# One prompt pair loaded a stage earlier, one row tile of two projections loaded without a free buffer, and the last stores split over two queues

## What is computed

```
# layer 0
qa, ka, va, za, qb, kb, vb, zb = split(rmsnorm(x) @ w_in_even)     # 3584 columns
oa = dilated sliding-window attention(qa, ka, va)    # 8 heads of 64, causal; prompt, and sample over a cache
ob = retention(rotary(qb), rotary(kb), vb)           # 4 heads
x  = x + concat(oa * silu(za), head_norm(ob) * silu(zb)) @ w_out_even
# layer 1
q, kc, vc, ks, vs, kw, vw, gl, z = split(rmsnorm(x) @ w_in_odd)    # 2864 columns
o  = gated sum of compressed, selected and window attention(q, ...)   # 16 heads
x  = x + (o * silu(z)) @ w_out_odd
y  = rmsnorm(x)
```

## Time and profile before

| what | value |
|---|---|
| median of three runs | 1970.13 us |
| the profiled execution, its own time | 1969.05 us |
| span of its instructions | 1967.3 us |
| TensorE busy | 95% of the span, 13566 matmuls |
| VectorE, ScalarE, GpSimd busy | 44%, 36%, 20% |
| DMA | 254.06 MB, 129 GB/s on average |
| mean granted TensorE clock | 0.978 of 2.4 GHz |

### The profile page before, as it was taken

How to read it: one execution, slowest core, us unless ns; L and a number is a source line. 1 busy time by engine, 2 the same in 40 slices (tenths; PEclk the granted TensorE clock), 3 DMA queues, 4 the chain that set the end, 5 groups by cost and what they waited for, 6 DMA issues and landing times. The chain is left out here.

```text
span 1967.3 us, 35219 instructions
## 1 busy us (share of the span) xinstructions
PE 1878.1 (95%) x13566; PEld 1449.7 (74%) x13566; DVE 865.5 (44%) x2575; ACT 699.5 (36%) x1527; POOL 390.6 (20%) x552
## 2 busy tenths in 40 slices
PE   7999999798998999999999999999899999999898
PEld 6777777576876888788885555565688778788787
DVE  5222221576555353212411121212677777777534
ACT  5100000464332231001003323322567676776522
POOL 0000000000751000000022113110355555555200
PEclk9999999899997999999989999999899999999999
DMA  5443442663788653844345143250400000000464
GB/s 206 163 145 128 147 142 72 217 192 104 251 274 262 196 199 120 257 168 146 85 177 191 44 151 119 76 151 12 124 23 23 7 23 24 23 13 7 156 203 144
DMA packets 158532, 254.06 MB, mean 129 GB/s; under 512 B 33858, under 2 KB 109824, under 8 KB 154016
## 3 DMA queue, kind: packets, MB, share of 16 engines
q1 hardware_dynamic: 144480, 206.25, 32.3%
q0 software_dynamic: 4608, 33.56, 4.8%
q10 hardware_dynamic: 9280, 12.00, 2.0%
HBM read 205.85 MB, written 52.96 MB: 132 GB/s over the span
## 5 line engine op out<-in xcount | busy, mean ns | idle before, releaser
L1717 POOL TENSOR_SCALAR sparse_pr<-sparse_pr,sparse_coef,sparse_gate 128x63 f32<-128x63 f32 (+8 forms) x384 | 247.2, 666 | 206.9 <-DVE sparse_coef L1671 206.8
L1059 PE MATMUL x_acc<-x_w_hi,x_y_lo 128*128 128x478 f32 (+3 forms) x768 | 274.9, 358 | 2.4 <-DVE x_y_lo L907 2.4
L1059 PE MATMUL x_acc<-x_w_lo,x_y_hi 128*128 128x478 f32 (+3 forms) x768 | 269.2, 350 | 0.0
L1059 PE MATMUL x_acc<-x_w_hi,x_y_hi 128*128 128x478 f32 (+3 forms) x768 | 268.7, 350 | 0.0
L2865 PE MATMUL ss_ps_h<-ss_xT,cmp_w 128*128 128x508 f32 x512 | 244.0, 594 | 0.8 <-ACT ss_xT L2707 0.8
L1613 ACT ACTIVATE sparse_pr<-sparse_pr,sparse_nmax 128x63 f32<-128x63 f32 (+8 forms) x384 | 227.4, 597 | 2.8 <-DVE sparse_nmax L1665 2.8
L447 PE MATMUL h_acc<-h_w_hi,h_y_lo 128*128 128x512 f32 x448 | 177.6, 396 | 0.8 <-DVE h_y_lo L372 0.8
L447 PE MATMUL h_acc<-h_w_hi,h_y_hi 128*128 128x512 f32 x448 | 174.8, 390 | 0.0
L447 PE MATMUL h_acc<-h_w_lo,h_y_hi 128*128 128x512 f32 x448 | 174.8, 390 | 0.0
L1059 PEld LDWEIGHTS x_acc<-x_w_hi,x_y_lo 128*128 128x128 f32 x768 | 145.7, 190 | 29.2 <-issue 14.7
L1059 PEld LDWEIGHTS x_acc<-x_w_hi,x_y_hi 128*128 128x128 f32 x768 | 145.6, 190 | 11.3
(11 more groups left out here) (383 smaller groups left out, 2667.8 us busy)
## 6 DMA issues: line engine op xcount, KB each, us to landing
h<-h_out SPq DMA_DIRECT2D x56, 256.0 KB, 2.1
h_w_side<-in_even_w_in SPq DMA_DIRECT2D x16, 896.0 KB, 5.0
h_w_raw<-in_even_w_in SPq DMA_DIRECT2D x6, 2048.0 KB, 7.9
x_w_side<-in_odd_w_in SPq DMA_DIRECT2D x16, 716.0 KB, 4.7
cmp_lent<-in_odd_w_in SPq DMA_DIRECT2D x5, 1912.0 KB, 9.1
h<-x_out SPq DMA_DIRECT2D x40, 239.0 KB, 2.2
ev_unit<-in_cache_a_k SPq DMA_DIRECT2D x4, 2048.0 KB, 8.4
ev_unit<-in_cache_a_v SPq DMA_DIRECT2D x4, 2048.0 KB, 12.1
```

The lines of the kernel that those rows point to most:

```text
L1059: last = nc.tensor.matmul(acc[b][:, 0:passes[p][3]], left[:, k, t * P:(t + 1) * P], weights(right, p)[:, k, :], start=(k == 0 and a == 0), ...
L1717: nc.gpsimd.tensor_scalar(row, row, one, gate[:, t, 2 * i + e, (br + 1) % 3:(br + 1) % 3 + 1], ALU.mult, ALU.mult).then_inc(scaled, 1)
```

## The change

- **First pair.** Queries, keys and values of the first dilated pair and the table of constants are loaded within `project`, by SyncE, behind the second store of the last chunk, once the stores of chunks 0 to 2 have landed. They go into a memory (`cmp_lent`) that the projection doesn't use. Two probability buffers of the dilated stage that lay there have tiles of their own now, and `oT` and `o_sb` of that stage move into the memory that held the constants.
- **Third row tile.** In both output projections row tile 2 is loaded into `held[2]` and `held[3]`, with a semaphore of its own (`third_in`), and without a wait, as the first thing that SyncE does. Tile 4 then waits for tile 0 to be turned, not for tile 2.
- **Last stores.** In both `attend_prompt` the last group is copied out in pieces with a semaphore for each (`out_done`), and its four stores go out two by SyncE and two by ScalarE (`store_last`).
- **Warm calls.** `project` and both `attend_prompt` begin on ScalarE with one activation of 128x1 (Sqrt, Exp) whose result isn't used.

```diff
+class FirstPair:
+    def __init__(self, nc, ctx, constants, h):
+        self.lent = ctx.enter_context(nc.sbuf_tensor("cmp_lent", [P, 2 * PAST], F32))
+        part = [self.lent[:, m * T:(m + 1) * T] for m in range(4)]
+        self.q_in, self.k_in, self.v = (x.rearrange("p (t c) -> p t c", t=NT) for x in part[0:3])
+        self.con, self.con_in = constants(ctx, "dilated", part[3]), sem("con_in")
...
+    def load(self, sp):
+        for to, col, loaded in ((self.q_in, QA, self.q_loaded), (self.k_in, KA, self.kv_loaded), (self.v, VA, self.v_loaded)):
+            sp.dma_start(to, self.hp[:, :, col:col + P]).then_inc(loaded[0], 16)
+        self.con.load(sp, self.con_in)
...
                     for t in range(NT):
                         store(i, t)
+                        if i == n_chunks - 1 and t == 1:
+                            n_needed = -(-pair.last_column // chunk) * NT
+                            for b in range(3):
+                                sp.wait_ge(stored[b], 16 * ((n_needed - b + 2) // 3))
+                            pair.load(sp)
...
                 act.wait_ge(eps_ready, 1)
+                nc.scalar.activation(warm[:, :], eps[:, :], ACT.Sqrt)
...
         def loads_of(t):
-            return t // 2 * 16 * len(gates)
+            if t == 2:
+                return third_in, 16 * len(gates)
+            return loaded[t % 2], (t // 2 - (1 if t % 2 == 0 else 0)) * 16 * len(gates)
+
+        def x_of(t):
+            return held[2] if t == 2 else x[:, t % 2, :]
+
+        def z_of(t):
+            return held[3] if t == 2 else z[:, t % 2, :]
...
                 def load_gated(t, n):
-                    b = t % 2
-                    if t >= 2:
-                        sp.wait_ge(turned[b], t // 2)
-                    sp.dma_start(x[0:n, b, :], rows(src, t, n)).then_inc(loaded[b], 16)
+                    done = loads_of(t)[0]
+                    if t > 2:
+                        sp.wait_ge(turned[t % 2], 1 if t == 4 else t // 2)
+                    sp.dma_start(x_of(t)[0:n, :], rows(src, t, n)).then_inc(done, 16)
...
+        def store_last(eng, m):
+            i, t, at = units[4 * last_group + m][0:3]
+            eng.wait_ge(out_done, at % 4 + 1)
+            eng.dma_start(mix[t * P:(t + 1) * P, i * P:(i + 1) * P], o_sb[last_group % 2][:, at % 4, :]).then_inc(stored[last_group % 2], 16)
...
                     ins = nc.vector.tensor_scalar(to[:, c0:c0 + HD], src[:, c0:c0 + HD], coef[u % N_COEF][:, e:e + 1], None, ALU.mult)
-                ins.then_inc(bank_free[entry_of[what, x] % RING], 1)
+                    if x == last_group and e == 1:
+                        ins.then_inc(out_done, 1)
...
+            if what == "out" and x == last_group:
+                for m in range(4):
+                    nc.vector.tensor_copy(to[:, m * P:(m + 1) * P], src[:, m * P:(m + 1) * P]).then_inc(out_done, 1)
...
-                    load_pair(sp, 0)
-                    con.load(sp, con_in)
                     load_pair(sp, 1)
-                    load_v(sp, 0)
                     load_v(sp, 1)
...
+                    if g == last_group:
+                        for m in (0, 2):
+                            store_last(sp, m)
+                        continue
...
+                nc.scalar.activation(warm[:, :], con("ident")[:, 0:1], ACT.Exp)
...
+                for m in (1, 3):
+                    store_last(act, m)
```

More of the change, by code:

```diff
@@ L555, in project_out @@
         gain_in, eps_ready = sem("gain_in"), sem("eps_ready")
-        loaded = [sem(f"loaded{b}") for b in range(2)]
+        loaded, third_in = [sem(f"loaded{b}") for b in range(2)], sem("third_in")
         opened = first if early is None else early
@@ L1041, in turn @@
                         pe.wait_ge(yT_written[b], u)
[L1042 removed]
+                    fr = z[:, t % 2, :] if second else x_of(t)
                     for k in range(KD):
[L1044 removed]
+                        last = nc.tensor.transpose(tps[b][:, k, 0:n], fr[0:n, k * P:(k + 1) * P], ident[0:n, 0:n])
                     last.then_inc(turned[b], 1)
@@ L1343, in attend_prompt @@
         else:
-            con, con_in = constants(ctx, kind, outer.constants), sem("con_in")
-            q_in = [sb(f"q_in{b}", [P, NT, P]) for b in range(2)]
+            con, con_in = outer.pair.con, outer.pair.con_in
+            q_in = [outer.pair.q_in, sb("q_in1", [P, NT, P])]
         qT = [sb(f"qT{b}", [P, T]) for b in range(2)]
-        if sparse:
-            pr = [sb(f"pr{b}", [P, 2, rows[b % 2]]) for b in range(UB)]
-        else:
-            pr = [outer.wide[b // 2][:, 0:2 * rows[0]].rearrange("p (e c) -> p e c", e=2) if b in (0, 2) else
-                  sb(f"pr{b}", [P, 2, rows[b % 2]]) for b in range(UB)]
+        pr = [sb(f"pr{b}", [P, 2, rows[b % 2]]) for b in range(UB)]
         prT = [sb(f"prT{b}", [P, 512]) for b in range(N_T)]
+        warm = sb("warm", [P, 1])
         nmax = [sb(f"nmax{b}", [P, NC]) for b in range(UB)]
@@ L1356, in attend_prompt @@
         coef = [sb(f"coef{b}", [P, NC]) for b in range(N_COEF)]
-        oT = [sb(f"oT{b}", [P, 512]) for b in range(2)]
-        o_sb = [sb(f"o{b}", [P, 4, P]) for b in range(2)]
+        if sparse:
+            oT = [sb(f"oT{b}", [P, 512]) for b in range(2)]
+            o_sb = [sb(f"o{b}", [P, 4, P]) for b in range(2)]
+        else:
+            oT = [outer.z[:, 0, b * 512:(b + 1) * 512] for b in range(2)]
+            o_sb = [outer.z[:, 1, b * 512:(b + 1) * 512].rearrange("p (t c) -> p t c", t=4) for b in range(2)]
         if sparse:
```

50 lines of the change are left out of this document (28 added, 22 removed).

## The result

| | before | after |
|---|---|---|
| median of six runs | 1968.83 us (1965.8 to 1970.44) | 1952.92 us (1950.6 to 1959.13) |
| profiled execution, own time | 1969.05 us | 1950.6 us |
| its span | 1967.3 us | 1948.7 us |
| its mean granted clock | 0.978 | 0.981 |

The ratio is 0.9923, with a 95% interval of 0.991 to 0.9937: 0.77% faster, 15.9 us between the medians. The spans of the two profiled executions lie 18.6 us apart; the profiled one of after is the fastest of its six.

What follows compares the result with a forecast made beforehand. TensorE is busy in 95% of the span, so time is won only where it stands still or runs at the lower clock. Terms 3.9 + 0.8 + 2.2 + 7.1 + 3.5 = 17.5 us off 1969.05 gave 1952 us, range 1949 to 1955.5.

Steps and rivals of the forecast that it cites:

- One sign that the prediction named for being wrong: Output projections: a wait for DMA-fed rows before tile 3 or 5 would show the prediction wrong.
- first pair: Dilated start: early loads let TensorE start 3.56 us earlier and remove a 0.31 us keys wait; together 3.9 us.
- warm calls: Dilated start: the 1.28 us table load moves to the barrier; 0.8 us, bounds 0 and 1.28; kernel and sparse starts 0.
- last stores: Ends of both attention stages: two queues and stores by quarters save 1.3 us (dilated) and 0.9 us (sparse), 2.2 together.
- first projection: First output projection: waits of 1.84 and 2.06 us and 3.4 of slow clock go, less 0.2: 7.1 us.
- TensorE starts at about 349.73: Dilated start: with the data already there, TensorE starts right behind the barrier, 3.56 us earlier.
- about 6 us of work run at half clock: Dilated start: slow work worth 3 us if the clock returned at once, as much the other way if later; taken as 0.
- It just fits: First output projection: at 5.8 us of load, tile 5 is in at 634, and TensorE needs it at 634.2.
- no wait, no fall ... 1.7 us lost each: First output projection: without its two waits the clock stays up, saving 1.7 us at each, 3.4 in sum.
- The waits did move in part: Rival: the output projections' waits move to the next tile, half of 10.6 us comes, gain 12.2, 1957 us; chance 0.2.
- The dilated stage gave nothing back: Rival: dilated stage starts earlier but gives it back, bound by ScalarE and VectorE; gain 12.8, 1956 us; chance 0.07.
- The loads in flight together: Slower rival: loads of tile 3, tile 4 and weights share engines, tile 3 lands last; 1971 us or more; chance 0.03.

Runs made afterwards that it cites:

- number 1: Changed kernel, but the first dilated pair and its constants are loaded behind the barrier again: 1959.78 us, ratio 0.9951 to the kernel before.
- number 4: Changed kernel without the three small activations that load a table early: 1953.62 us, ratio 0.9918 to the kernel before.
- number 5: Changed kernel, but both output projections ask for the second weights behind tile 5, not ahead of it: 1957.48 us, ratio 0.9948 to the kernel before.
- number 9: Kernel before, with only the third row tile of both output projections loaded early: 1962.06 us, ratio 0.9953.
- the fill: Changed kernel plus 14 unread TensorE products behind the first projection's last product: 1950.92 us, ratio 0.9918; run again, 1952.79 us, 0.9912.

## Why the prediction was right, and where a term was not

Forecast 1952, measured 1952.92. The sum was 17.5 us from the trace. By the measured stretches it should have been 16.2 (the front 5.4, which holds the first two terms of the table, and the others as they stand there), and the medians are 15.9 apart. That the forecast comes within 1 us is in part luck: 2.6 us too much in the first projection stood against 1.1 us that was in no term and 0.4 of the first pair. One sign that the prediction named for being wrong did come: a wait for loaded rows before tile 5, 1.64 us. The time was right, and that step of its reasoning was not.

| term | forecast | measured | from |
|---|---|---|---|
| first pair | 3.9 | 4.3 | front, number 1 |
| warm calls | 0.8 | 0.7 to 1.2 | number 4; fronts before (27.2) and of number 1 |
| last stores | 2.2 | 2.0 | 5.54 to 4.12, 4.68 to 4.10 |
| first projection | 7.1 | 4.5 | first pass |
| second projection | 3.5 | 3.2 | its stretch to the end |
| wait ahead of the first projection | none | 1.1 | chance, below |

*First pair.* The step "TensorE starts at about 349.73" came out in its mechanism, with the barrier as releaser, but 3.98 us behind the last product and not 3.6: the warm calls cost that 0.32 us (number 4). The clock's share was put at 0 with bounds of 3 us, and within them it is a draw. Seven fronts of the same work spread over 2.4 us, and the order follows the clock, which is low in them for 3.4 us (the shortest) to 10.2 (the four longest). The reading "about 6 us of work run at half clock" was short: before, the clock fell only 2.3 us into the gap, so 4.9 of the 13.7 low us were idle and 8.8 were work. Not foreseen was that a gap of 4 us can leave the turns at 2.4 GHz.

*Warm calls.* I took 0.8 between 0 and 1.28, on the ground that another engine would take some of the 1.04 us. None did; the size is right because the later barrier takes 0.32 us back, which was not foreseen. The drain that the Trainium skill, "ScalarE: Activation LUTs", section "What ACT_TABLE_LOAD costs", adds to the load would have made the term 1.4 larger. The trace of number 4 speaks against it: without the warm call the load is back, and what returns in TensorE's waits is 1.04 us, less than even the load's own 1.28. The start of the kernel gave 0, as argued from the waits for DMA: the first product starts at 14.89 without and at 14.93 with the call.

*Last stores.* The size was right, and part of the reason wrong. I counted issue times of two queues and an earlier start as if they added up. They replace each other: 0.65 and 1.16 us by themselves at the dilated end, 1.42 together; 0.61 and 0.35 at the sparse end, 0.58 together. At the sparse end the four copies last 0.89 us and the single one 0.69, and VectorE has other work behind them that ends 0.8 us ahead of the barrier; that this eats the earlier start is argued and not shown.

*First projection: the term that was mis-sized.* Two steps failed. "It just fits" for tile 5: the load took 7.6 us and not 5.8, since the weights ahead of it were still on their way, and number 5 shows that this lateness passes to whatever tile stands behind them. An earlier issue doesn't help it: the changed kernel issued tile 5 13.9 us behind the pass's first turn and its repetition 16.0 us, and both times its silu began 21.5 us behind that turn. And "no wait, no fall ... 1.7 us lost each": the clock did stay up where the waits had been, but the 3.4 us were added as if TensorE set the pace alone. It doesn't here. The first pass of the changed kernel lasts 39.50 us with the clock low for its first 2.8 us and a wait of 1.64, and in its second run 39.52 us with the clock low for 9.1 us and no wait for rows at all. Where the clock is high TensorE meets the late tile, where it is low the tile is there. The ten profiles with the early third tile and the old place of the weights order themselves so: low for 2.8 us, wait 1.64; 4.3, 1.33; 4.4, 1.14; 7.9, 0.90; 8.2 to 9.1 in the six others, none. In eleven profiles with the early third tile the first pass lasts 39.1 to 40.4 us, 39.7 in the mean; without it 44.78 and 43.66. So 2.6 of the 7.1 us were not there to be won.

```profile
605.00:615.00 10.00, 9.35 (x39) 0.55 0.90 303
615.00:625.00 10.00, 10.00 (x72) 1.00 0.94 323
```

These are windows of the second run of the changed kernel: 0.55 of the clock with the transfers at a share of 0.90, and then full clock beside a share of 0.94.

*What was not in the sum.* The wait ahead of the first output projection is 2.66 us in the profiled execution. In the ten others that have the changed kernel's dilated end, or nearly so, it is 2.94, 3.07, 3.12, 3.31, 3.36, 3.84, 3.96, 4.18, 4.60 and 5.19, and in the two of the old kernel's kind 4.87 and 4.59. No edit orders these numbers, but the stage's last eight issues do, the stores of the sample states: where they took 8.8 to 9.7 us the wait is 2.7 to 3.4, where they took 10.0 to 10.4 it is 3.8 to 5.2 (before and number 9 among these), and TensorE starts 4.0 to 4.2 us behind the end of the last issue in twelve of the thirteen profiles, 3.5 in the other. What makes these issues short or long isn't shown. The mean of the wait moved by 1.1 us (4.7 to 3.7), which so few profiles can't tell from chance. The 2.7 us by which the two traces overstate the gain are made up by chance at several places. Against the means of the profiles the two traces show 0.8 us too much up to the last product of `project`, 0.5 in the front, 1.1 in this wait, 0.8 in the first pass, and 0.6 too little in the second projection.

*Rivals.* The waits did move in part, to tile 5 (1.64 us): half of that rival, inside the forecast's own range. The dilated stage gave nothing back: from the row that ends the front to the last turns of the stage it is 108.08 us in both kernels. The loads in flight together slowed each other a little: from issue to silu tiles 3 and 4 of the first projection took 6.5 and 6.4 us, and 6.1 and 5.6 before. TensorE waited for neither.

## What to carry to other kernels

Price a wait and the slow clock beside it as one thing where transfers run at a share near 1: what the clock gave back there, the next late tile took. Here the tile behind the large load in one queue was the late one, and shifting the load by one place shifted the wait; that fewer bytes or an earlier load of the weights would remove it was not tried. A few products that nobody reads, shorter than the barrier, kept the clock at all three barriers where they were tried. They won time only at the one behind which TensorE itself set the pace (2.8 us); at the two behind which it soon waited for VectorE or for rows they won nothing. So ask first who sets the pace behind the barrier. And take no price from one profile's clock or one profile's wait at a barrier: the same program moved by 1 to 2 us there.

## What the runs showed of the hardware that was not expected

- The moment at which the clock falls behind TensorE's last product is not fixed: 2.1, 2.3, 2.4, 2.4, 2.5, 2.7, 2.9, 2.9, 3.5, 5.3 and 5.3 us in the eleven profiles without the fill (read from the granted clock of stretches of one microsecond). In the last two TensorE had been at work again for over 1 us when it fell. With 3.3 us of products in a gap of 4.2 us it did not fall at all, twice.
- One program's profiled execution had the first 2.8 us of the output projection at 1.2 GHz and its repetition 9.1 us, with the same length of the pass.
- The clock came back with nothing but turns behind a standstill. In the changed kernel TensorE stood 2.66 us and did 16 turns from 603.85 to 607.14; the clock was 0.50 at their start, 0.69 from 606 to 607 and 1.00 from 607 on. In the kernel before the turns began at 614.08, and the clock was 0.50 up to 618 and 0.97 from 618 to 619, with the first product at 618.38.
- With the warm calls the barrier at the dilated start opened 0.32 us later, 3.94 us behind the last product in place of 3.62.
- The issue of the last stores counts little once it overlaps VectorE's work: started by quarters, four issues in one queue or two in each of two differ by 0.26 us in what the barrier waits for, where one issue takes 0.44 us; when all four wait for VectorE's last piece, they differ by 0.65 us (both at the dilated end).
